# Gate with x as the moving operand; FFN input projections with both parts of x in one matmul, and a sum over two PSUM banks behind it

## The reference

```python
def swiglu(x, w_in, w_out):
    a, b = jnp.split(x @ w_in, 2, axis=-1)
    return (jax.nn.silu(a) * b) @ w_out

gate = jax.nn.sigmoid(x @ w_gate)     # NSA: 16 heads x 3 branches = 48 columns
```

## Time and profile before

| | |
|---|---|
| median of 3 runs | 1678.3 us (1677.15 to 1678.34) |
| profiled execution, its time | 1673.66 us |
| its span, first to last instruction | 1671.9 us |
| granted clock, mean over the span | 0.995 |
| PE busy | 1638.1 us, 98% |
| DVE busy | 1094.7 us, 65% |
| ACT busy | 918.8 us, 55% |
| POOL busy | 159.3 us, 10% |

### The profile page before, as it was taken

One profiled execution on the slowest core, in us unless ns is written; L12 is line 12 of the kernel. 1 busy time (PEld: TensorE's weight loads), 2 busy tenths in 40 slices (PEclk: granted clock), 3 DMA queues, 4 the chain that ended last, 5 costly groups with the idle time before them and its releaser, 6 DMA issues.

```text
span 1671.9 us, 30723 instructions
## 1 busy us (share of the span) xinstructions
PE 1638.1 (98%) x13324; PEld 1551.5 (93%) x13324; DVE 1094.7 (65%) x1371; ACT 918.8 (55%) x1248; POOL 159.3 (10%) x63
## 2 busy tenths in 40 slices
PE   7999999999999999999999899999999999999999
PEld 7999989999999989998987699998999898799998
DVE  6888868664665567765578856656655567665554
ACT  6966778455544455444477844444444447764432
POOL 0000000000022101220000002210222000002210
PEclk9999999999999999999999899999999999999999
DMA  7554433554355465555642235546554564335544
GB/s 265 184 184 156 149 140 138 191 178 154 134 196 182 154 201 208 194 169 169 212 152 102 102 124 192 189 149 205 202 198 151 185 226 134 120 130 198 194 156 129
DMA packets 44630, 284.03 MB, mean 170 GB/s; under 512 B 4944, under 2 KB 6608, under 8 KB 17744
## 3 DMA queue, kind: packets, MB, share of 16 engines
q1 hardware_dynamic: 44352, 281.99, 48.9%
q10 hardware_dynamic: 144, 0.08, 0.0%
HBM read 281.00 MB, written 1.05 MB: 169 GB/s over the span
## 4 chain that ended last, share of the span: by engine, by line
PE 83%; DVE 7%; ACT 6%; issue 2%; DMA 0%; DVEq 0%; ACTq 0%
PE bank L509 83%; ACT WH L1156 2%; DVE WL L1741 2%; DVE STAT L1886 1%; ACT SB L1279 1%; DVE HT L1797 0%; PE bank L660 0%; ACT XR L1163 0%; ACT XM L1163 0%; DVE XM L1749 0%; DVE SB L1883 0%; ACT FB L1180 0%; DVE FB L1767 0%; DMA PAR<-in_par 0%; DVE FA L2182 0%
## 5 line engine op out<-in xcount | busy, mean ns | idle before, releaser
L1741 DVE TENSOR_TENSOR WL<-RAW,WH 128x2048 fp32r<-128x2048 f32 (+1 forms) x282 | 590.3, 2096 | 271.3 <-ACT WH L1156 271.1
L509 PE MATMUL bank<-XR,WH 128*128 128x256 f32 x3648 | 651.1, 282 | 10.9 <-DVE WL L1928 10.4
L1156 ACT ACTIVATE WH<-RAW 128x2048 fp32r<-128x2048 f32 (+1 forms) x282 | 493.1, 1752 | 213.4 <-PE bank L509 208.7
L509 PEld LDWEIGHTS bank<-XR,WH 128*128 128x128 f32 x3648 | 560.5, 189 | 15.4 <-DVE WL L1928 10.4
L509 PE MATMUL bank<-XR,WL 128*128 128x256 f32 x1824 | 511.4, 280 | 0.0
L509 PEld LDWEIGHTS bank<-XR,WL 128*128 128x128 f32 x1824 | 345.4, 189 | 0.0
L509 PE MATMUL bank<-XF,WH 128*128 128x512 f32 x880 | 305.3, 392 | 0.0
L509 PE MATMUL bank<-XM,WH 128*128 128x256 f32 x1664 | 294.8, 281 | 3.3 <-DVE XM L1749 1.8
L509 PEld LDWEIGHTS bank<-XM,WH 128*128 128x128 f32 x1664 | 254.3, 188 | 4.8 <-DVE XM L1749 2.8
L509 PE MATMUL bank<-XF,WL 128*128 128x256 f32 x880 | 246.2, 280 | 0.0
L509 PE MATMUL bank<-XM,WL 128*128 128x256 f32 x832 | 233.0, 280 | 0.0
(11 more groups left out here) (278 smaller groups left out, 1647.0 us busy)
## 6 DMA issues: line engine op xcount, KB each, us to landing
RAW<-in_f1i SPq DMA_DIRECT2D x44, 1024.0 KB, 4.9
RAW<-in_f2i SPq DMA_DIRECT2D x44, 1024.0 KB, 4.9
RAW<-in_w_in SPq DMA_DIRECT2D x35, 1024.0 KB, 4.9
RAW<-in_w_ffn_in SPq DMA_DIRECT2D x22, 1024.0 KB, 4.9
RAW<-in_f1o SPq DMA_DIRECT2D x32, 704.0 KB, 4.1
RAW<-in_f2o SPq DMA_DIRECT2D x32, 704.0 KB, 4.2
RAW<-in_diff_w_in SPq DMA_DIRECT2D x12, 1024.0 KB, 5.0
RAW<-in_w_ffn_out SPq DMA_DIRECT2D x16, 704.0 KB, 4.1
```

The costliest lines, as they stand in the source:

```text
L509: return e.matmul(o, l, r, start=start, stop=stop)
L1156: e.activation(split_at(u, cols)[0], RAW[:, u % NRAW, 0:cols], ACT.Copy).then_inc(hi_done.tick(u), 1)
L1741: e.tensor_tensor(lo, RAW[:, u % NRAW, 0:cols], hi.bitcast(f32), sub).then_inc(lo_done.tick(u), 1)
```

## The change

**FFN input.** `unit_wide` takes the place of `unit_T` in the five FFNs. Half m of a unit gets a bank of its own, and a group is now two matmuls: `WH` with both planes of x (512 columns, whole bank) and `WL` with the high plane (256 columns, first half). The kind "wide" hands out the bank pairs 4-5, 2-3, 0-1 in turn. `join` on DVE (a TENSOR_REDUCE over the two halves of both banks, 1024 values to 512 a partition) brings the result to SBUF, and the products that read the bank before now read SBUF. `norm_sum` of an FFN uses banks 6 and 7.

**Order of splits.** In the FFN loop `asked((w_in, c + 1))` comes ahead of `high_part` (ACT) and `low_part` (DVE).

**Gate.** The weights stand still now (128 columns read at a step of 48, of which the first 48 count) and x moves, 256 columns, 8 groups of three, woven into unit 6: pieces 0 to 5 of unit 6, pieces 0 to 5 of the gate, piece 6 of each, piece 7 of each, then `norm_sum`. ACT copies the result to SBUF and PE turns it with two transposes behind unit 0 (`gate_turn`).

**Diff stage.** The turn of the kinds "main" and "pair" is set at its start.

The PSUM banks are declared as one tensor, so that `join` can read two of them at once.

```diff
@@ -256,7 +256,8 @@
         COS, SIN = E0[:, 0:256], E0[:, 256:512]
         SH = EA.rearrange("p (h c) -> p h c", c=384)
         SHb = SH[:, :, :].rearrange("p h (b c) -> p h b c", c=128)
-        banks = [ctx.enter_context(nc.psum_tensor(f"bank{i}", [128, 512], f32)) for i in range(8)]
+        BANKS = ctx.enter_context(nc.psum_tensor("bank", [128, 8, 512], f32))
+        banks = [BANKS[:, i, :] for i in range(8)]
         SQ, RS, T2 = TMP[:, 0, :], TMP[:, 1, :], TMP[:, 2, :]
 
 
...
@@ -489,7 +491,7 @@
 
         def tensor(e, counting):
             q = Queue(e, counting)
-            kinds = {"main": (0, 1, 2), "open": (3,), "aux": (4, 5, 6, 7), "pair": (0, 1), "held": (2, 3), "one": (0,), "three": (1, 2, 3, 0), "first": (1,), "second": (2,),
+            kinds = {"main": (0, 1, 2), "wide": (4, 5, 2, 3, 0, 1), "last": (6, 7), "open": (3,), "aux": (4, 5, 6, 7), "pair": (0, 1), "held": (2, 3), "one": (0,), "three": (1, 2, 3, 0), "first": (1,), "second": (2,),
                      "third": (3,), "four": (0, 1, 2, 3)}
             turn = dict.fromkeys(kinds, 0)
             emptied = {}
@@ -585,9 +587,23 @@
                     t.then_inc(used.tick(u), 1)
                     empties(key, event(2 * n + 1))
 
-            def norm_sum(stage):
-
-                b = take("aux", ("norm", stage))
+            def unit_wide(name, x, stage, order=in_time):
+
+                u, w = weights(name)
+                bs = [take("wide", (name, "wide", m)) for m in range(2)]
+                xv = x[:, :, :].rearrange("p z (k t) -> p z k t", t=256)
+                for m, k in sorted(((m, k) for m in range(2) for k in range(8)), key=lambda mk: order(*mk)):
+                    q.wait_ge(parts, (stage, k))
+                    wh, wl = at_k(w, k, m * 128, 128)
+                    mm(tiles(bs[m], 256), wh, xv[:, :, k, :], k == 0, False)
+                    t = mm(bs[m][:, 0:256], wl, xv[:, 0, k, :], False, k == 7)
+                t.then_inc(used.tick(u), 1)
+                for m in range(2):
+                    empties((name, "wide", m), (joined, name))
+
+            def norm_sum(stage, kind="aux"):
+
+                b = take(kind, ("norm", stage))
                 q.wait_ge(small["con"], 0)
                 q.wait_ge(acc, (stage, "all"))
                 t = mm(b[:, 0:256], ones128, ACC[:, 0:256])
@@ -600,12 +616,12 @@
                 empties(("norm", stage), (rinv, stage))
 
             def ffn(stage, w_in, w_out):
-                x = two(XN[stage])
+                turn["wide"] = 0
                 for c in range(11):
-                    unit_T((w_in, c), x, stage, 8, (rscaled, (stage, c)), order=in_time if c else in_order_of_x)
+                    unit_wide((w_in, c), XN[stage], stage, in_time if c else in_order_of_x)
                     if c == 0:
-                        norm_sum(stage)
-                    unit_T((w_in, 11 + c), x, stage, 8, (ffn_mul, (stage, c)))
+                        norm_sum(stage, "last")
+                    unit_wide((w_in, 11 + c), XN[stage], stage)
                 av = XF[:, :, :].rearrange("p z (k t) -> p z k t", t=256)
                 for m in range(8):
                     b = take("main", (w_out, "sum", m))
@@ -967,17 +983,42 @@
                     t = mm(b[:, r * 256:r * 256 + 256], BDV[:, G, r, :], PCT[:, G, :], False, r == 1)
                 t.then_inc(cmp_pe.tick(("out", G)), 1)
 
-            name = ("nsa_gate", 0)
-            u, w = weights(name, 48, 384)
-            b = take("main", name)
-            for j, k in sorted(((j, k) for j in range(2) for k in range(8)), key=lambda jk: in_order_of_x(*jk)):
-                q.wait_ge(parts, ("mix_0", k))
-                t = mm2(b[:, j * 48:j * 48 + 48], at_k(xT, k, j * 128, 128), at_k(w, k, 0, 48), k == 0 and j == 0, k == 7 and j == 1)
-            t.then_inc(used.tick(u), 1)
-            empties(name, (sig1, ("gate", 1)))
+            def gate_columns(b, k0, k1):
+
+                u = U[("nsa_gate", 0)]
+                q.wait_ge(lo_done, u)
+                wh, wl = split_at(u, 464)
+                for k in range(k0, k1):
+                    q.wait_ge(parts, ("mix_0", k))
+                    at = slice(k * 48, k * 48 + 128)
+                    t = mm2(b[:, 0:256], (wh[:, at], wl[:, at]), at_k(xT, k, 0, 256), k == 0, k == 7)
+                if k1 == 8:
+                    t.then_inc(used.tick(u), 1)
+                    empties(("nsa_gate", 0), (copied, "gate"))
+
+            def gate_turn():
+                b = take("aux", "gate")
+                q.wait_ge(copied, "gate")
+                for j in range(2):
+                    t = e.transpose(b[:, j * 128:j * 128 + 128], RS[:, j * 128:j * 128 + 128], ident)
+                t.then_inc(cmp_pe.tick("gate"), 1)
+                empties("gate", (sig1, ("gate", 1)))
+
+            name = ("nsa_w_in", 6)
+            u, w = weights(name)
+            b, g = take("main", name), take("main", ("nsa_gate", 0))
+            for k0, k1 in ((0, 6), (6, 7), (7, 8)):
+                for m in range(2):
+                    for k in range(k0, k1):
+                        q.wait_ge(parts, ("mix_0", k))
+                        t = mm2(b[:, m * 256:m * 256 + 256], at_k(w, k, m * 128, 128), at_k(xT, k, 0, 256), k == 0 and m == 0, k == 7 and m == 1)
+                if k1 == 8:
+                    t.then_inc(used.tick(u), 1)
+                    empties(name, (rscaled, ("k", 0)))
+                gate_columns(g, k0, k1)
             norm_sum("mix_0")
-            nsa_unit(6, ("k", 0), "main")
             nsa_unit(0, ("q", 0), "main")
+            gate_turn()
             nsa_sum(("k", 0))
             nsa_unit(8, ("k", 1), "main")
             nsa_sum(("q", 0))
@@ -1072,6 +1113,7 @@
             def diff_out(n, k0, k1, kind="pair"):
                 out_part("diff_w_out", n, two(XO), "od", 4, k0, k1, lambda k: (hrow, ("diff", k)), kind)
 
+            turn["main"], turn["pair"] = 0, 1
             diff_unit(0, "main")
             norm_sum("mix_1")
             diff_unit(4, "main")
@@ -1254,6 +1296,8 @@
                     o = half(F(3), c % 4)
                     q.wait_ge(rscaled, (stage, c))
                     e.activation(o, o, ACT.Silu).then_inc(silu.tick((stage, c)), 1)
+                    if c < 10:
+                        asked((w_in, c + 1))
                     q.wait_ge(ffn_mul, (stage, c))
                     high_part((stage, "act", c), half(F(4), c % 4), XF, c * 512, 512)
                 e.preload_act_table_set("natural_log_exp_and_others")
@@ -1580,17 +1624,19 @@
 
             asked(("nsa_gate", 0))
             rsqrt_mean("mix_0")
+            q.wait_ge(used, U[("nsa_gate", 0)])
+            copy("gate", RS[:, 0:256], in_bank(("nsa_gate", 0))[:, 0:256])
             asked(("nsa_w_in", 6))
-            q.wait_ge(used, U[("nsa_gate", 0)])
+            nsa_square(("k", 0))
             q.wait_ge(cols, "ncol")
+            q.wait_ge(cmp_pe, "gate")
             for j in range(2):
-                e.activation(gates[:, j * 48:j * 48 + 48], in_bank(("nsa_gate", 0))[:, j * 48:j * 48 + 48], ACT.Exp,
+                e.activation(gates[:, j * 48:j * 48 + 48], in_bank("gate")[:, j * 128:j * 128 + 48], ACT.Exp,
                              scale=ncol[:, j:j + 1]).then_inc(sig1.tick(("gate", j)), 1)
             q.wait_ge(sig1, ("gate", 1))
             e.activation(gates, gates, ACT.Ln, bias=con("one")[:, 0:1]).then_inc(sig2.tick("gate"), 1)
             q.wait_ge(sig2, "gate")
             e.activation(gates, gates, ACT.Exp, scale=-1.0).then_inc(gated.tick("gate"), 1)
-            nsa_square(("k", 0))
             asked(("nsa_w_in", 0))
             nsa_root(("k", 0))
             nsa_square(("q", 0))
@@ -1818,6 +1864,14 @@
                         add_block(stage, k, in_bank((name, n, "half", m))[:, 0:256], 1.0, before)
                         chunk_lo(after, k)
 
+            def join(name, dst):
+
+                at = BANK[name, "wide", 0]
+                q.wait_ge(used, U[name])
+                b = BANKS[:, at:at + 2, :]
+                e.tensor_reduce(tiles(dst, 256), b.rearrange("p m (z t) -> p m t z", z=2), X, add).then_inc(joined.tick(name), 1)
+                q.wait_ge(joined, name)
+
             def ffn(stage, w_in, w_out, before, after, factor):
                 asked((w_in, 0))
                 if stage == "ffn1_0":
@@ -1830,15 +1884,20 @@
                     o, p = half(F(3), c % 4), half(F(4), c % 4)
                     if c >= 4:
                         q.wait_ge(sr_done, (stage, c - 4))
-                    scale((stage, c), U[(w_in, c)], o, stage)
+                    join((w_in, c), o)
+                    q.wait_ge(rinv, stage)
+                    e.tensor_tensor(tiles(o, 256), tiles(o, 256), r_of(stage), mult).then_inc(rscaled.tick((stage, c)), 1)
                     asked((w_in, 11 + c))
                     if stage == "ffn1_0" and c < 8:
                         q.wait_ge(rstd, "final")
```

(8 more changed lines are left out.)

## The result

The changed kernel takes 1665.34 us (median of 6 runs, 1663.26 to 1666.09) against 1677.36 of the kernel before (6 runs, 1674.72 to 1678.34) beside it: ratio 0.9927, 95% interval 0.9917 to 0.9936. That is 12.0 us less; the forecast was 11.3 less and 1667.0 us. The profiled execution took 1664.09 us, span 1662.3, mean clock 0.996.

What follows compares the result with a forecast made beforehand. PE's matmuls were taken to bound the FFNs, with half clock at the gate. FFN inputs 8.6 us plus NSA start 2.7 gave 11.3 us, so 1678.3 falls to 1667.0 us; range 1661 to 1673.

Steps and rivals of the forecast that it cites:

- the likeliest case: Whole kernel: the main forecast, 1667.0 us, given a chance of 0.62 and by itself 1663.5 to 1670.5 us.
- Chunks of 11.09 us in all five FFNs: FFN input projections: chunks shorten from 11.20 to 11.31 us to 11.09, 8.6 us in all, at least 6.0.
- an edge between input and output: FFN, from input to output projections: no stall by half a microsecond; at a join of 1.8 us, 0.1 us each.
- Join 1.2 us, DVE fits: FFN chunks: each join takes 1.2 us, DVE's chunk becomes 9.05 of 11.09 us and stays hidden under PE.
- The rival with DVE as the bound: FFN chunks: a join of 2.4 us makes DVE's chunk 11.5 us, the kernel slower at 1705.8 us; chance 0.05.
- The earlier `asked` gains nothing on PE: FFN loop: weight splits are needed two units later and hidden by some 4 us, so moving them earlier gains nothing.
- POOL and the products: FFN scale and product, now with two SBUF inputs: might block with POOL, 1.1 us a block; none expected.
- NSA start, 2.7 us: Start of the NSA stage: DVE's first loop step comes 2.7 us earlier; bounds 1.0 to 4.5 us.
- Both new waits: NSA stage's start: PE waits 0.7 us for unit 6's low part and 1.0 us for the sum of k's squares.
- Banks: nothing: Diff stage and aux banks: the new bank order costs nothing, as no PE wait for a bank stands out.
- Second stretch of half clock, +-3 us: Late in the NSA stage: shifted timing may make the half-clock stretch go or grow, worth +-3 us.
- The carry-over of 4.6 us: Whole kernel: the median lies 4.6 us above the profiled execution's time, and this gap was kept for the changed kernel.

Runs made afterwards that it cites:

- x11: Kernel before with only the earlier splits of the FFN loop added (old narrow form, gate and banks): 1675.27 us, ratio 0.9997.
- x10: Changed kernel with both joins of each FFN chunk done twice, the extra results unused: 1681.17 us, ratio 1.0011.
- x4: Changed kernel with the FFN loop's splits back in the old order, behind high and low part: 1673.11 us, ratio 0.9981.
- x1: The changed kernel run again without any edit, as common base of the follow-ups: 1664.92 us, ratio 0.9928.
- x2: Kernel before with only the wide FFN input form, joins and diff-stage bank setting; old gate and split order: 1676.85 us, ratio 1.0001.
- x12: Changed kernel with the old split order and the second FFN's final hidden-state product cut from 256 values to 8: 1670.53 us, ratio 0.9967.
- x8: Kernel before with 256 instead of 48 moving columns in each gate matmul, same order: 1673.20 us, ratio 0.9983.
- x5: Changed kernel with the diff stage's fourth output unit taking its banks from "pair", bank 1 first: 1665.51 us, ratio 0.9934.
- x3: Kernel before with only the new gate: 1672.54 us, ratio 0.9971.
- x9: Changed kernel with the join of each FFN chunk's first unit done twice, the extra result unused: 1665.33 us, ratio 0.9920.
- x6: Changed kernel with gate pieces 0 to 5 ahead of unit 6 and norm_sum ahead of its last two pieces: 1662.75 us, ratio 0.9920.

## Why the prediction was right, and where its steps were not

The time came within 1.7 us, inside the range, and so did the likeliest case. Part of that closeness is luck: in the traces the change gives 9.6 us where 11.3 were forecast, and the medians give 12.0 for a reason that has nothing to do with the forecast's terms (last point below). By its steps:

- **Chunks of 11.09 us in all five FFNs: right.** The form's distance, read from the output sums, held everywhere, and the excess of the last three FFNs went with the old form; x11 shows that this excess comes and goes in the old form with no change of its matmuls, so its 2.6 us of the term could have been another number. The term was 8.6 us and measured 8.0: 1.10, 1.12, 1.79, 2.28 and 1.74 us, stage by stage, each about 0.1 less than eleven chunks would give. The prediction named an edge between input and output that might cost 0.1 us a stage; it isn't that, since PE has no wait there in any of the five FFNs. What it is stays open.
- **Join 1.2 us, DVE fits: right** (1.22; no wait of PE in a chunk). The rival with DVE as the bound was put at a join of 2.3 us. In x10 DVE had 2.4 us a join, and four FFNs were still just under PE's chunk: the point is about right for them, and nearly all of the loss came in the second FFN. The rival's price was far too high, 1705.8 against x10's 1681.17: DVE's pace at such a join is 10.99, not 11.5, so there is hardly any loss in four FFNs (and 0.3 x 55 is 16.5, not 18).
- **"The earlier `asked` gains nothing on PE": the step that failed.** It gains 8.2 us (x4 against x1; 9.0 in the trace), as much as the whole FFN term. Without it the wide form gives nothing (x2, 1.0001). The prediction added up DVE's durations in the new order (10.6 us with L1838's product, "still fits"; measured 10.17 where DVE leads) and never laid out the old order, where the same work has 1.8 us of waits for ACT in it. The sum came out right since both parts were in the change; the reason given for one of them was wrong.
- **POOL and the products: right.** The scale and the product take 0.69 us each. The sentence on L1838's product was right in kind: x12 shows that it lasts until POOL is done. The Trainium skill, "SBUF — State Buffer", section on who interferes with whom, calls this an exclusive lock between a DVE instruction with two SBUF inputs and a GpSimd one that reads SBUF. The trace agrees: 8 values took 1.26 us.
- **NSA start, 2.7 us: measured 3.2** for DVE's step of the loop (37.55 to 34.37) and 3.5 for PE's, as worked out. Both new waits came, 0.58 for 0.7 and 0.85 for 1.0. x8 shows that the clock alone is 2.75 of it.
- **"Banks: nothing": right in time.** A wait of 1.7 us for a bank did appear (output units 0 and 1 now have banks 1 and 0, so unit 3's first half meets the bank of unit 1), but it costs nothing: what sets that end is DVE's and ACT's chain from the last sums to the next FFN's x (x5).
- **Second stretch of half clock, +-3 us: right as a bound.** It stayed at 10.24 us in the NSA stage; one of 3.4 us stood in the diff stage and cost 1.5. It is not the change's: x11 and x3, with the old FFNs and banks, have it too, and x10, with the change, does not. Within the NSA stage, the five executions with a stretch some 136 us behind the stage's start have a rest of 135.9 to 136.4 us, and the nine without one there have 133.4 to 134.3, whatever the kernel. Counted from the loop's first step, DVE's rows in x9 are 0.9 us behind those of x6 ahead of that stretch and 2.5 us behind it.
- **The carry-over of 4.6 us** from profile to median: the changed kernel's median stands only 1.25 us above its profile. That is why the medians fall by 2.4 us more than the spans. The profiled execution of the kernel before, 1673.66 us, was faster than every other one of that kernel in this set (the lowest is 1673.70), and the carry-over took that as a rule. Half clock explains little of it: its mean clock is 0.9947, that of the 23 executions beside x1 0.9942 on average, which at 0.8 us for each 0.001 is 0.4 us. The rest stays open; so do the 2 us by which x3's median gained more than its gate.

## What to carry to other kernels

Where work is moved on an engine that "fits", lay out its list with the waits for the engines beside it, in the old order as in the new: busy time per chunk says too little, as 10.35 us of work had a pace of 12.16. Two edits of one change can be worth nothing alone (x2, x11) and 8 us together (the five FFNs of the changed kernel), so undo each one by itself before giving a reason for it. Before a difference of 1 or 2 us in a stage is explained by a wait, set the stages of several kernels beside each other by their half-clock stretches: here that turned the obvious cause, a new wait of 1.7 us for a bank, into none.

## What the hardware showed that was not expected

- While PE ran 48 matmuls with 48 moving columns, back to back at 112 ns, its granted clock fell to 0.50 (1.2 GHz) and stayed there for 6.83 us, without an idle stretch of PE ahead of it; the same 48 with 256 columns kept 1.00 (2.4 GHz) and took 5.7 us in place of 6.07. More columns made the kernel 3.1 us faster.
- A DVE product of 8 values took 1.26 us and one of 256 took 1.53, as both lasted until POOL's multiplication ended (by 0.02 and 0.28 us past it).
- Half-clock stretches of 3.4, 6.8, 10.2 and 13.7 us came in the NSA stage at places that differ from execution to execution, 3.4 to 17 us in all in its second part; one of 3.4 us in the diff stage, always 98 to 100 us behind its start, cost 1.5.
- The same group of three matmuls of 256 columns takes 350 ns in one FFN and 353 in another, and the first FFN went from 350 to 353 (chunks of 11.20 and 11.31 us for 32 groups) when only the order of the splits on ACT and DVE was changed (x11).
